# Decoder trunk on one core: the mix stage reordered and overlapped with the last attention pair, and three smaller edits

## The reference

```python
for l in range(2):
    h = rms_norm(x, mix_norm_g[l]);  u = h @ w_in[l]
    y_mla = mla_group(...)      # 8 heads of causal attention, swept in 128-query blocks
    y_ssm = mamba2_group(...)   # state space scan in 8 chunks of 128 tokens, times silu(z), RMS norm
    y_lru = rglru_group(...)    # gated linear recurrence (LRU)
    y_mix = concatenate([rms_norm(y_mla, mla_out_g[l]), y_ssm, rms_norm(y_lru, lru_out_g[l])])
    x = x + y_mix @ w_out[l]
    x = x + memory_cross_attention(rms_norm(x, ...), rms_norm(mem, ...), w_mq, w_mk, w_mv, w_mo)
    x = x + square(relu(rms_norm(x, ...) @ w_mlp1[l])) @ w_mlp2[l]
return rms_norm(x, final_norm_g)
```

## Time and profile before

| what | value |
|---|---|
| median of 3 runs | 2988.43 us (2987.38 to 2990.2) |
| profiled execution, its own time | 2983.76 us |
| its span, first to last instruction | 2982.0 us |
| PE busy | 2876.7 us, 96% |
| DVE, ACT, POOL busy | 51%, 30%, 51% |
| mean granted clock of TensorE | 0.994 of full speed |
| chain that ended last | PE 83%, DVE 6%, ACT 4%, POOL 4% |

### The profile page before, as it was taken

One profiled execution on the slowest core, in us unless ns is written; L12 is line 12 of the kernel. 1 busy time (PEld: TensorE's weight loads), 2 busy tenths in 40 slices (PEclk: granted clock), 3 DMA queues, 4 the chain that ended last, 5 costly groups with the idle time before them and its releaser, 6 DMA issues.

```text
span 2982.0 us, 36852 instructions
## 1 busy us (share of the span) xinstructions
PE 2876.7 (96%) x13290; PEld 2228.4 (75%) x13290; DVE 1535.4 (51%) x1944; ACT 879.9 (30%) x1449; POOL 1534.1 (51%) x1138
## 2 busy tenths in 40 slices
PE   8999989999999999999999999899999999999998
PEld 6765557887878888888887555588878788888886
DVE  7584446204574555545585644551145655455555
ACT  3445563224130111111225555522233211111113
POOL 3332223350487777777644222243414877777776
PEclk9999999999999999999999999999999999999998
DMA  3100011230111111111110000112201111111112
GB/s 131 47 9 5 1 43 40 74 106 7 46 45 47 46 56 56 49 46 46 57 67 33 9 5 1 49 44 92 85 12 45 43 56 51 46 44 56 56 53 74
DMA packets 61423, 140.37 MB, mean 47 GB/s; under 512 B 9232, under 2 KB 11280, under 8 KB 60688
## 3 DMA queue, kind: packets, MB, share of 16 engines
q1 hardware_dynamic: 61328, 139.06, 13.5%
HBM read 134.58 MB, written 4.46 MB: 47 GB/s over the span
## 4 chain that ended last, share of the span: by engine, by line
PE 83%; DVE 6%; ACT 4%; POOL 4%; issue 2%; DMA 1%; SPq 0%; POOLq 0%; DVEq 0%; ACTq 0%
PE ps L1214 22%; PE ps L1198 18%; PE ps L761 17%; PE ps L1071 6%; PE ps L959 3%; PE ps L989 2%; PE ps L1126 2%; PE ps L1150 2%; PE ps L865 1%; PE ps L816 1%; PE ps L1102 1%; PE ps L975 1%; PE ps L1086 1%; DVE xbc L1680 1%; POOL ring L677 1%
## 5 line engine op out<-in xcount | busy, mean ns | idle before, releaser
L1214 PE MATMUL ps<-hm_h,ring 128*128 128x512 f32 x2048 | 641.5, 391 | 6.8 <-DVE hm_l L1987 4.8
L1995 DVE TENSOR_TENSOR x<-ps,x 128x512 f32<-128x512 f32 x512 | 351.7, 689 | 274.0 <-PE ps L1214 273.8
L674 POOL TENSOR_TENSOR ring<-raw,ones 128x512 fp32r<-128x512 f32 x338 | 354.1, 1048 | 261.5 <-PE ps L1214 203.0
L1214 PEld LDWEIGHTS ps<-hm_h,ring 128*128 128x128 f32 x2048 | 384.3, 188 | 101.2 <-issue 16.6
L677 POOL TENSOR_TENSOR ring<-raw,ring 128x512 fp32r<-128x512 f32 x338 | 439.0, 1299 | 26.5
L761 PE MATMUL ps<-hA,wsp 128*128 128x512 f32 x1920 | 442.9, 392 | 0.0
L761 PEld LDWEIGHTS ps<-hA,wsp 128*128 128x128 f32 x1920 | 360.4, 188 | 80.3 <-issue 6.1
L553 POOL TENSOR_TENSOR wsp<-raw,ones 128x1024 fp32r<-128x1024 f32 x67 | 131.6, 1964 | 552.8 <-PE ps L761 496.6
L1214 PE MATMUL ps<-hm_l,ring 128*128 128x512 f32 x1024 | 398.8, 389 | 0.0
L1198 PE MATMUL ps<-hT,ring 128*128 128x512 f32 x1440 | 331.9, 389 | 1.5 <-POOL ring L677 1.5
L1198 PEld LDWEIGHTS ps<-hT,ring 128*128 128x128 f32 x1440 | 270.1, 188 | 58.4 <-POOL ring L677 2.3
(11 more groups left out here) (272 smaller groups left out, 3830.6 us busy)
## 6 DMA issues: line engine op xcount, KB each, us to landing
raw<-in_weight_tiles SPq DMA_DIRECT2D x248, 256.0 KB, 2.5
raw<-in_weight_tiles SPq DMA_DIRECT2D x112, 512.0 KB, 3.2
outT<-x SPq DMA_DIRECT2D x16, 256.0 KB, 2.1
x<-in_xT SPq DMA_DIRECT2D x3, 1024.0 KB, 10.5
wh<-in_head_weights SPq DMA_DIRECT2D x8, 256.0 KB, 2.6
mem_s<-in_memT SPq DMA_DIRECT2D x2, 1024.0 KB, 4.8
x<-in_xT SPq DMA_DIRECT2D x2, 512.0 KB, 5.6
lw_s<-in_lru_gates SPq DMA_DIRECT2D x2, 256.0 KB, 7.4
```

Of the source, the lines that this page charges most:

```text
L674: pool.tensor_tensor(ring[:, slot, 0, :], blk(i), ones[:, 0:1].to_broadcast([P, HT]), ALU.mult).then_inc(op_ready[slot], 1)
L1214: last = pe.matmul(ps[:, bank, :], w[:, part, k, (m % 2) * P:(m % 2 + 1) * P], h[k][:, cols_of(half)], start=(k == 0 and part == 0 and h i ...
L1995: dve.tensor_tensor(xm, ps[:, bank, :], xm, ALU.add).then_inc(x_add, 1)
```

## The change

1. **Side order of the last pair.** The chunks 6 and 7 have their tasks at steps 0 to 6 and 7 to 12 instead of 3 to 8 and 11 to 15. DVE's squares of z (`sq`, `ss`) move from behind the attention into step 62.
2. **Earlier operands.** The first two tiles of `w_out` are loaded from unit 48 on into attention memory that is free by then, and split by POOL (`split_early`) between its tasks of the last pair; POOL also splits the LRU output (`split_lru`), which ACT and DVE did before.
3. **The mix stage.** The last square sum of the attention output moves from POOL to DVE. ACT does the three Ln together and then the three Exp. PE does the two tiles of round `R_OUT` together, k by k, the LRU chunks first.
4. **EL and EA** are two float32r matmuls each, with `aU` as a high and a low part, both built by POOL.
5. **Start of the attention.** The value blocks go to other banks (`V_BANK`, `V_AFTER`), the rotated query half of head 1 has a buffer of its own, and the first scores wait for five value blocks and for the keys of the first pair alone.
6. **Smaller ones.** The sums for the cross attention's norm, and its 1/rms, one tile earlier; the two Ln and the two Exp of the compressed queries and keys together.

```diff
+        if c == PAIRS - 1:
+            plan = [(0, "EL", a), (1, "RB", a - 1), (2, "EA", a), (3, "CB", a), (4, "TR", a), (6, "Y", a),
+    (7, "EL", a + 1), (8, "EA", a + 1), (9, "RB", a), (10, "CB", a + 1), (11, "TR", a + 1),
+    (12, "Y", a + 1)]
...
+MIX_ORDER = (6, 7, 4, 5, 0, 1, 2, 3)
+MIX_SLOT = ((2, 3, 4, 5, 12, 14, 10, 11), (6, 7, 13, 15, 0, 1, 8, 9))
+V_BANK = (2, 4, 5, 7, 0, 6, 1, 3)
+V_AFTER = {1: (2, 0), 2: (4, 0), 3: (6, 2), 4: (7, 3), 6: (8, 4)}
...
-        aU = at("aU", G1, [P, SH, P])
+        aU = [at("aU_hi", G1, [P, SH, P], F32R), at("aU_lo", SPL + 13 * K + 512, [P, SH, P], F32R)]
...
+    sp.wait_ge(s_ps, here(s_ps, UNITS - 2 * NBLK))
+    for s in range(2):
+        sp.dma_start(raw_early[:, s, :], wt[layer, 2 * R_OUT + s, :, :]).then_inc(raw_ready[s], 16)
     sp.wait_ge(o_ps, here(o_ps, 2 * PAIRS * 2))
-    load_pair(R_OUT, 2 * R_OUT)
+    load_pair(R_OUT + 1, 2 * R_OUT + 2)
...
+        for part, a in enumerate((att_h, att_l)):
+            pool.tensor_tensor(aU[part][:, :, :], tri_le[:, :].unsqueeze(1).to_broadcast([P, SH, P]),
+                               a[:, h, :].bitcast(F32).unsqueeze(2).to_broadcast([P, SH, P]), ALU.mult)\
+                .then_inc(m_aU, 1)
...
+        turned = sq if head == 1 else q_tmp
+        pool.tensor_tensor(q[NOPE:DQ, :], q[NOPE:DQ, :], turned[NOPE:DQ, :], ALU.add).then_inc(q_rope, 1)
...
+    def split_early(s, dst):
+        pool.wait_ge(raw_ready[s], here(raw_ready[s], R_OUT * 16 + 16))
+        pool.tensor_tensor(dst[:, 0, :], raw_early[:, s, :], ones[:, 0:1].to_broadcast([P, TILE]),
+                           ALU.mult).then_inc(w_ready[s], 1)
+        pool.wait_ge(w_ready[s], here(w_ready[s], R_OUT * 2 + 1))
+        pool.tensor_tensor(dst[:, 1, :], raw_early[:, s, :], dst[:, 0, :].bitcast(F32),
+                           ALU.subtract).then_inc(w_ready[s], 1)
+        pool.wait_ge(w_ready[s], here(w_ready[s], R_OUT * 2 + 2))
+        pool.sem_inc(raw_free[s], 1)
+    def split_lru(n):
+        hi, lo = mixed[:, MIX_SLOT[0][6 + n], :], mixed[:, MIX_SLOT[1][6 + n], :]
+        pool.tensor_copy(hi, gt_s[:, n, :]).then_inc(mix_gt, 1)
+        pool.wait_ge(mix_gt, here(mix_gt, 2 * n + 1))
+        pool.tensor_tensor(lo, gt_s[:, n, :], hi.bitcast(F32), ALU.subtract).then_inc(mix_gt, 1)
...
+        if c == PAIRS - 1:
+            split_early(0, w_early)
+            split_lru(0)
+            split_lru(1)
...
-    y_square(2 * PAIRS - 1)
-    pool.wait_ge(o_ps, here(o_ps, 4 * PAIRS))
-    with pool.Fori(R_OUT, R_X) as i:
+    split_early(1, wsp[:, 1, :, :])
+    split(R_OUT + 1, 0, o_ps, 4 * PAIRS)
+    split(R_OUT + 1, 1, t_ready[1], R_OUT + 1)
...
-        if b >= 2:
-            pe.wait_ge(ip_a, here(ip_a, (2, 4, 5, 6, 7, 8)[b - 2]))
-        if b >= 4:
-            pe.wait_ge(ip_v, here(ip_v, b - 3))
-        pe.matmul(ps[:, (b + 2) % 8, :], ckv_s[:, b * P:(b + 1) * P], wv_s[:, :],
+        if b in V_AFTER:
+            pe.wait_ge(ip_a, here(ip_a, V_AFTER[b][0]))
+            if V_AFTER[b][1]:
+                pe.wait_ge(ip_v, here(ip_v, V_AFTER[b][1]))
...
+        def of_terms(constant):
+            for part in range(2):
+                last = pe.matmul(ps[:, 7, :], constant, aU[part][:, :, :].rearrange("p h t -> p (h t)"),
+                                 start=part == 0, stop=part == 1)
+            last.then_inc(side_ps, 1)
...
-            pe.wait_ge(v_done, here(v_done, NBLK))
-            pe.wait_ge(k_rope, here(k_rope, 4))
+            pe.wait_ge(v_done, here(v_done, 5))
+            pe.wait_ge(k_rope, here(k_rope, 2))
...
-    pe.wait_ge(side_a, here(side_a, act_reads(len(SIDE) - 1)))
-    for j, src in enumerate((sq, ss, acc)):
-        pe.wait_ge(mix_sum, here(mix_sum, min(j + 1, 2)))
-        if j == 2:
+    for j, (src, bank) in enumerate(((sq, 4), (ss, 6), (acc, 0))):
+        if j < 2:
+            pe.wait_ge(mix_sum, here(mix_sum, j + 1))
+        if j == 1:
+            pe.wait_ge(side_a, here(side_a, act_reads(len(SIDE) - 1)))
+            pe.wait_ge(y_done, here(y_done, 2 * PAIRS))
+        elif j == 2:
+            pe.wait_ge(s_exp, here(s_exp, UNITS))
             pe.wait_ge(y_acc, here(y_acc, 2 * PAIRS))
         for half in range(2):
-            last = pe.matmul(ps[:, 2 * j + half, :], ones[:, 0:1].to_broadcast([P, P]), src[:, cols_of(half)],
+            last = pe.matmul(ps[:, bank + half, :], ones[:, 0:1].to_broadcast([P, P]), src[:, cols_of(half)],
                              start=True, stop=True)
         last.then_inc(mix_col, 1)
...
+    def mix_products(s, at_k, w_part, part):
+        w = (w_early[:, w_part, :], wsp[:, 1, w_part, :])[s]
+        k = MIX_ORDER[at_k]
+        for half in range(2):
+            last = pe.matmul(ps[:, 2 * s + half, :], w[:, k * P:(k + 1) * P], of_mixed(part, k, half * HT, HT),
+                             start=(at_k == 0 and w_part == 0 and part == 0),
+                             stop=(at_k == DC - 1 and part == 1))
+        return last
+    pe.wait_ge(mix_gt, here(mix_gt, 4))
+    for s in (1, 0):
+        pe.wait_ge(w_ready[s], here(w_ready[s], R_OUT * 2 + 2))
+        pe.wait_ge(t_free[s], here(t_free[s], U_OUT + 1))
+        if s == 0:
+            pe.wait_ge(mix_ln, here(mix_ln, 1))
+        for at_k in range(2):
+            for w_part, part in ((0, 0), (0, 1), (1, 0)):
+                mix_products(s, at_k, w_part, part)
+    for at_k in range(2, DC):
+        pe.wait_ge(mix_hi, here(mix_hi, at_k - 1))
+        for s in range(2):
+            for w_part in range(2):
+                mix_products(s, at_k, w_part, 0)
+        pe.wait_ge(mix_lo, here(mix_lo, at_k - 1))
+        for s in range(2):
+            last = mix_products(s, at_k, 0, 1)
+            if at_k == DC - 1:
+                last.then_inc(t_ready[s], 1)
+    pair(R_OUT + 1, U_OUT + 1, of_mixed)
     pe.wait_ge(mem_sum, here(mem_sum, 1))
     pe.matmul(ps[:, 6, 0:NMEM], ones[:, 0:1].to_broadcast([P, P]), rs[:, 0:NMEM],
               start=True, stop=True).then_inc(mem_col, 1)
...
-        if n == 2:
+        if n == 1:
             means(N_XA, ss, 6)
+        elif n == 2:
...
-    rstd_of(N_CQ, QR, 4).then_inc(norm_done, 1)
-    rstd_of(N_CKV, KVR, 6).then_inc(norm_done, 1)
+    for i, width, bank in ((N_CQ, QR, 4), (N_CKV, KVR, 6)):
+        act.wait_ge(mean_ps, here(mean_ps, i + 1))
+        link(log_mean(banks(bank), banks(bank), width))
+    for bank in (4, 6):
+        act.activation(banks(bank), banks(bank), ACT.Exp, scale=-0.5).then_inc(norm_done, 1)
...
+    logs = (banks(4), banks(6), rs[:, :])
+    for j, (sums, width) in enumerate(((banks(4), SI // SG), (banks(6), SI // SG), (banks(0), HEADS * DV))):
         act.wait_ge(mix_col, here(mix_col, j + 1))
-        rstd(banks(2 * j), banks(2 * j), width).then_inc(mix_rstd, 1)
-    for n, (k, src) in enumerate(((4, z_s[:, 0, :]), (5, z_s[:, 1, :]), (0, y_mla[:, 0, :]),
-                                  (1, y_mla[:, 1, :]), (2, y_mla[:, 2, :]), (3, y_mla[:, 3, :]))):
+        ins = log_mean(logs[j], sums, width)
+        link(ins) if j < 2 else ins.then_inc(mix_ln, 1)
+    def mix_scale(j):
+        act.activation(logs[j], logs[j], ACT.Exp, scale=-0.5).then_inc(mix_rstd, 1)
+    def mix_high(n, src):
         act.wait_ge(mix_n, here(mix_n, n + 1))
-        if n == 2:
-            act.wait_ge(mix_lo, here(mix_lo, 4))
-        act.activation(hB[:, 0, k, :], src, ACT.Copy).then_inc(mix_hi, 1)
+        act.activation(mixed[:, MIX_SLOT[0][MIX_ORDER[2 + n]], :], src, ACT.Copy).then_inc(mix_hi, 1)
+    mix_scale(0)
+    mix_scale(1)
+    mix_high(0, z_s[:, 0, :])
+    act.wait_ge(mix_ln, here(mix_ln, 1))
+    mix_scale(2)
+    mix_high(1, z_s[:, 1, :])
+    for n in range(4):
...
+    rstd_of(N_XA, D, 6, rs[:, :]).then_inc(bc_done, 1)
     high(2)
     high(3)
-    rstd_of(N_XA, D, 6, rs[:, :]).then_inc(bc_done, 1)
...
+    link(dve.tensor_copy(att_h[:, :, :], att[:, :, :]))
+    link(dve.tensor_tensor(att_l[:, :, :], att[:, :, :], att_h[:, :, :].bitcast(F32), ALU.subtract))
...
+        if n == UNITS - 2:
+            dve.wait_ge(m_z, here(m_z, NBLK))
+            for j, out in enumerate((sq, ss)):
+                dve.tensor_tensor(out[:, :], z_s[:, j, :], z_s[:, j, :], ALU.mult).then_inc(mix_sum, 1)
...
+    y_last = y_mla[:, PAIRS - 1, HT:T]
+    link(dve.tensor_tensor(ysq[:, :], y_last, y_last, ALU.mult))
+    dve.tensor_tensor(acc[:, HT:T], acc[:, HT:T], ysq[:, :], ALU.add).then_inc(y_acc, 1)
...
+    scale_z(0)
+    scale_z(1)
+    mix_low(0, z_s[:, 0, :])
+    scale_y(0)
+    mix_low(1, z_s[:, 1, :])
     for n in range(4):
+        if n < 3:
+            scale_y(n + 1)
+        mix_low(2 + n, y_mla[:, n, :])
...
```

125 lines of the change are left out of this document (63 added, 62 removed), and 4 rows, old and new, of the table PER_LAYER.

## The result

The changed kernel takes 2947.55 us (median of 4 runs, 2946.57 to 2951.39) against 2987.9 us of before (4 runs, 2982.73 to 2990.2): a ratio of 0.987 with a 95% interval of 0.9853 to 0.9887, 40 us less. The prediction was 2952.4, in a range of 2938 to 2965. So the sign, the size and the range held. Two of its assumptions did not, that the clock stays up and that the median lies 4.7 us above the profiled execution, and they worked against each other.

The account below looks back on a forecast made before the run. PE bounds the kernel, busy 2876.7 of 2982.0 us. Per layer 13.0 + 2.5 + 2.9 + 1.3 - 1.7 = 18.0, twice 36.0, so 2988.4 - 36.0 = 2952.4 us, range 2938 to 2965.

Parts of the forecast that it names:

- the clock stays up: Mix stage: PE's clock stays at its upper level, being low only behind 6.5 us of idle; longest stop expected 1.5.
- the median lies 4.7 us above the profiled execution: Whole kernel: 2947.8 us forecast for the profiled execution, carried to the median of the runs by adding 4.7.
- The start: Attention's start: first scores and row maximum come earlier, DVE no longer standing 2.60 us for POOL; 2.9 us less per layer.
- EL and EA: Attention: each 0.41 us shorter, most of EL's gain waited away by outputs; 2.5 us less per layer, bounds 0 and 6.6.
- Cross attention: Cross attention: the wait of 1.36 us for 1/rms goes; 1.3 us less per layer.
- The mix stage: From RB's end to the second pair of tiles: 28.8 us instead of 41.8, 13.0 us less per layer.
- rival B: Mix stage stays DVE-bound; first mishap: POOL's split precedes DVE's last sum, 2 us late. 2964 us; 0.21 with D.
- The last pair: Attention's end: new order costs PE nothing, but POOL's wide work delays DVE's ce and sw; 1.7 us more per layer.
- The higher cost: Last pair: ce and sw each lose a whole POOL instruction, 5.2 us per layer; total 7.0 us higher, at 2959.
- A: Rival: DVE's operations slip between POOL's and EL's gain counts too; 22.2 us less per layer, 2944 us; chance 0.20.
- D: Rival: ACT's loads or z sums still follow RB, mix stage keeps half its wait; 2966 us; 0.21 with B.
- C: Rival: slower; DVE's squares of z wait for the last gate_z behind POOL's wide work; some 2995 us; chance 0.02.

Follow-up runs that it names:

- fill2: The changed kernel with needless float32r matmuls, as long as the stops, in PE's three stops at the attention's end: 2946.49 us.
- quiet: The changed kernel with both early weight tiles split before chunk 7, nothing wide on POOL while DVE makes ce, sw and xdd of chunk 7: 2945.93 us.
- poollate: The changed kernel with POOL's wide work of the last pair behind the last gate_z and DVE's squares of z behind the last reciprocals: 2953.34 us.
- tables: The changed kernel with Exp right behind its Ln for the state space sums in the mix stage, six table loads instead of two: 2962.57 us.
- seq: The changed kernel with the two tiles of the first output round one after the other behind the LRU products, not k by k together: 2956.83 us.
- qtmp: The changed kernel with one buffer for the rotated halves of head 0 and head 1, as before: 2955.19 us.
- el_f32: The changed kernel with EL and EA as plain float32 products of one aU, as before: 2952.41 us.

## Why the prediction was right, and where it was not

**The start, 2.9 predicted.** Measured 3.0 and 3.2, by the mechanism named (DVE's 2.60 behind POOL). What I left out is that with one buffer the new bank order puts DVE's stop ahead of four value blocks, as the run with one buffer shows.

**EL and EA, 2.5 predicted.** Measured 2.42 by the run that undoes this step alone, with EL's part waited away as named. The 2.54 from the old order is less clean, since other steps lie between those two kernels.

**Cross attention, 1.3 predicted.** Measured 1.6 and 1.8; the wait for `rs` is gone, and the other 0.3 to 0.5 is within what this stage varies from trace to trace (177.8 to 178.5 us in most layers).

**The mix stage, 13.0 predicted.** Measured 12.8 from RB's end to the second pair of tiles and 12.4 between the starts of the same PE instructions, the sounder figure; so the term was too large by 0.6 per layer. No run undoes the early operands or the moved last square sum alone, so how the gain divides among the steps is shown for the table loads, the k order and the side order only. The 0.6 ahead of z was 0.52, the 1.0 at the end 1.03, the k 2.72, and DVE's last sum got ahead of POOL's split by 0.31 us (429.25 against 429.56): rival B's first mishap did not come, but it was near. It did come in the runs with Y at step 15 and with the old order, where `acc` took 2.71.

**The last pair, 1.7 more predicted.** Measured 1.66 where the clock holds. That the total fits is luck. I had put all of it down to POOL beside `ce` and `sw`; the runs give that 1.1, and the other 0.6 belongs to the order itself, to which I had given nothing: the new stops of 0.59 and 1.48 replace one of 1.19, and a wait of 0.82 falls to 0.52. POOL's wide work was also smaller than the 13.7 us that I summed, 11.0, since two of the six operations are casts of 1.04. Operation by operation the bound held: `ce` lost 0.8 and `sw` 0.4, of at most 1.8 each. The higher cost, a whole POOL instruction for each, did not come: `ce` started at 400.05, when only the last 0.96 of POOL's subtraction (398.65 to 401.01) was left.

**The step that failed** is the clock. I wrote that it stays at its upper level, since the rows show it low only behind 6.5 us of idle time, and that the longest stop would be 1.5; and I set the last unit's uncovered transposes (some 1.4, measured 1.49) against the gaps before and put the balance at nothing on PE. The stops came as foreseen. What they did to the clock did not: 1.5 to 2.9 us per layer in which it fell, in the profiled execution 4.5 in all. That is more than the whole 3.5 between the 36.0 forecast and the 32.5 of the two traces; the other terms and the scatter at the start gave 1.0 back. The trace of before already spoke against my reading: in both layers its clock fell a second time, behind the waits of 1.99 and 1.97 us, as the window from 450 to 454 shows. I had looked at the window of the long stop alone and took it for a rule about all shorter ones. That stops of at most 1.5 us can do it, the trace of before does not show; its own two at the attention's end, 1.19 and 0.74, left the clock up in both layers.

**Why the median came out lower than the forecast, and not higher.** The sum was made against one trace and carried over to the medians with a fixed 4.7 us. But the runs of one kernel spread, and the spread goes with the granted clock: of the seven runs of before beside the run called fill2, the three with a mean clock of 0.994 took 2982.2 to 2984.3, the four with 0.991 or 0.992 took 2984.8 to 2990.6. The seven beside the one-buffer run divide in the same way, and those beside the changed kernel's repeat nearly so (one with 0.994 took 2987.1). In these three later sets the median of before is 2985.2, 2984.8 and 2983.0, from 0.8 below to 1.4 above the 2983.8 of its profiled execution, and not 4.7 above. Beside the first of them the repeat of the changed kernel is 34.9 us faster, close to the 36.0. Of the 5.4 us between this and the first comparison one half lies in the runs of before (2987.9 against 2985.2) and one in those of the changed kernel (2947.55 against 2950.33). So the gain is known to some us only, and that the median came out 4.9 below the forecast and not nearer to it is in part luck. Where in the kernel the longer runs lose their time stays open, since no trace shows them.

**The rivals.** None of them came. The median lies about halfway between the forecast and A, but A's mechanism is not there: EL's gain was swallowed, and `ce` and `sw` met POOL. Against B, the mix stage kept its pace by the thin margin. Against D, the loads are two, and the sums follow RB with no gap. C asked for POOL to be late by more than 10 us; `gate_z` of chunk 7 started at 411.35, with POOL idle for 7.23 us ahead of it. But a near relative of its mechanism is real: with Y three steps later the squares and then B's last sum met POOL's splits, and the mix stage took 5 to 6 us longer per layer, the clock included. The change as it stands avoids it by the place of two operations.

**Falls of the clock, counted.** In the runs that have the three bare stops (0.59, 1.48, 0.7) at the attention's end, the clock fell there in 10 of 16 layers: in both of the changed kernel and of the run quiet, in one of two of the repeat, poollate, tables, seq, qtmp and el_f32. In the runs where a filler, Y at step 15 or the old order stands there, it fell in none of 10, and in none of the two of before. If the stops made no difference, none of these 12 out of all 28 would be a chance of under 1 in 1000. So the stops bring it on, and whether it comes in a given layer is not settled by the program. Which of the three does it is not separated: with 1.48 cut to 0.24 and the other two left (Y at step 15) it stayed away. A layer pays nothing or 1.5 to 2.9 us for it.

## What to carry to other kernels

Cost a stop of the bounding engine not only at its own length: several stops of 0.6 to 1.5 us close together could drop TensorE's clock for what follows (in 10 of 16 layers here), and work that has to be done anyway is the filler. Where VectorE and GpSimd both read two operands from SBUF, give one of them a time when the other has none; here moving 11 us of POOL's work by a few steps was worth 1.1 us per layer and made a further reordering pay that had lost 5 us in all. And group ACT's functions by table before anything else in a normalisation that stands on the critical path: four loads of 1.28 us were worth 5.3 to 6.7 us per layer, with the clock. Last, take the windows at every stop of the trace before, not at the longest one alone: the fall behind 1.99 us stood in it.

## What the runs showed of the hardware that I had not expected

The clock fell to 0.50 with no stop longer than 1.49 us near it, and not in each layer with the same stops. The Trainium skill has a place for this (TensorE: Matmul & The Clock Gate, "A second HAM failure mode: psum-queue depth-cycling"): an engine that stands idle for short moments often enough can have its clock go down and up again without one long stop. The trace agrees in kind, with 5.98, 5.00 and 3.46 us for the same 32 matmuls.

The exclusion of DVE and POOL is paid by both in turns: DVE 2.90 and 3.37 for 1.2, POOL 3.22 for 2.35, in one stretch of 6 us. And it spreads: DVE's next two operations, late by it, took 1.89 and 2.71 for 0.69 each beside POOL's following split.

A float32 matmul of 512 columns, two rows of 0.43, is 3.8 times a float32r one of 0.227; a filler has to be chosen by that.
